# Recurrent mixer: triangular solve as 32x32 products joined by slot parity, low-rank products as 64x64 quarters in slots 33 and 35

## What is computed

```python
def rwkv_prepare(z, shift_w, w0, w_up, a0, a_up, k_k, k_a):
    ...
    w_log = -jax.nn.softplus(-(w0[:, None, None, :] + jnp.einsum('btr,drc->dbtc', jnp.tanh(wd), w_up))) - 0.5
    decay = jnp.exp(-jnp.exp(w_log.astype(jnp.float32)))
    a = jax.nn.sigmoid(a0[:, None, None, :] + jnp.einsum('btr,drc->dbtc', ad, a_up))
    ...
def wkv_scan(s0, scan_in):
    def step(s, inp):
        w, kk, a, k, v, r = inp
        sa = jnp.einsum('dbhij,dbhj->dbhi', s, kk)
        s = s * w[..., None, :] - sa[..., :, None] * (kk * a)[..., None, :] + v[..., :, None] * k[..., None, :]
        return s, jnp.einsum('dbhij,dbhj->dbhi', s, r)
    return lax.scan(step, s0, scan_in)
```

## Time and profile before

| | us |
|---|---|
| median of 3 runs | 4435.7 |
| the runs | 4431.9, 4435.7, 4444.6 |
| profiled execution, own time | 4427.0 |
| its span | 4425.4 |
| `rwkv_phase` in it | about 2085 to 2800 |
| one iteration of it (2249.21 to 2292.39) | 43.2 |

### The profile page before, as it was taken

One profiled execution on the slowest core, in us unless ns is written; L12 is line 12 of the kernel. 1 busy time (PEld: TensorE's weight loads), 2 busy tenths in 40 slices (PEclk: granted clock), 3 DMA queues, 4 the chain that ended last, 5 costly groups with the idle time before them and its releaser, 6 DMA issues. The chain is left out here.

```text
span 4425.4 us, 76116 instructions
## 1 busy us (share of the span) xinstructions
PE 3997.9 (90%) x30302; PEld 2848.3 (64%) x30302; DVE 2760.9 (62%) x5967; ACT 1446.1 (33%) x3210; POOL 900.1 (20%) x926
## 2 busy tenths in 40 slices
PE   7989999998999899998999999898999777778777
PEld 6747887755788687787888888686444333333332
DVE  5674433665533566755666666245777888888885
ACT  3353342344523335712444444322111111111111
POOL 1101110110201101110000000101344444444443
PEclk9999999999999999999999999898999999999999
DMA  4203443311443310131000000434999999999998
GB/s 127 86 30 109 154 141 99 103 36 39 157 144 128 117 57 20 63 132 51 19 18 26 24 18 6 151 111 164 388 409 420 416 415 415 409 409 417 412 415 334
DMA packets 149522, 795.01 MB, mean 180 GB/s; under 512 B 18808, under 2 KB 22120, under 8 KB 82352
## 3 DMA queue, kind: packets, MB, share of 16 engines
q0 software_dynamic: 84560, 574.75, 32.2%
q1 hardware_dynamic: 57120, 188.06, 13.0%
q10 hardware_dynamic: 7488, 27.30, 1.9%
HBM read 765.84 MB, written 20.00 MB: 178 GB/s over the span
## 5 line engine op out<-in xcount | busy, mean ns | idle before, releaser
L3224 PE MATMUL psum<-rows,diag 128*128 128x512 f32 x2048 | 1007.3, 642 | 226.7 <-ACT diag L3103 207.7
L3224 PEld LDWEIGHTS psum<-rows,diag 128*128 128x128 f32 x2048 | 410.4, 205 | 779.5 <-issue 765.9
L2922 POOL DMA_INDIRECT rows<-in_peer_uv,sel_idx x512 | 612.6, 1197 | 739.7 <-PE psum L3224 675.4
L2965 DVE SCALAR_TENSOR_TENSOR uh<-rows,h_rows 128x1024 f32<-128x1024 f32 x512 | 628.1, 1227 | 208.1 <-DMA rows<-in_peer_uv,sel_idx 183.1
L529 DVE TENSOR_TENSOR w_split_lo<-w_raw,w_split_hi 128x1024 fp32r<-128x1024 f32 (+1 forms) x271 | 326.2, 1214 | 497.6 <-ACT w_split_hi L516 493.2
L516 ACT CAST w_split_hi<-w_raw 128x1024 fp32r<-128x1024 f32 (+1 forms) x271 | 276.4, 1027 | 621.4 <-PE psum L465 396.7
L3096 ACT ACTIVATE g<-g 128x4 f32<-128x4 f32 x128 | 26.3, 205 | 1092.5 <-DVE g L2976 1092.5
L693 POOL TENSOR_TENSOR uT_lo<-normed_rows,uT_hi 128x512 fp32r<-128x512 f32 x64 | 90.2, 1410 | 661.2 <-ACT uT_hi L669 661.2
L465 PE MATMUL psum<-hT_mlp_hi,w_split_hi 128*128 128x512 f32 x512 | 201.3, 393 | 5.5 <-DVE hT_mlp_lo L261 5.5
L465 PE MATMUL psum<-hT_mlp_lo,w_split_hi 128*128 128x512 f32 x512 | 200.2, 391 | 0.0
L465 PE MATMUL psum<-hT_mlp_hi,w_split_lo 128*128 128x512 f32 x512 | 200.2, 391 | 0.0
(11 more groups left out here) (523 smaller groups left out, 8465.6 us busy)
## 6 DMA issues: line engine op xcount, KB each, us to landing
w_raw<-in_w_in SPq DMA_DIRECT2D x105, 512.0 KB, 4.1
w_raw<-in_w_up SPq DMA_DIRECT2D x64, 512.0 KB, 4.5
w_raw<-in_w_down SPq DMA_DIRECT2D x64, 512.0 KB, 4.4
amask_sb<-in_w_mod ACTq DMA_DIRECT2D x48, 512.0 KB, 3.7
wq<-in_peer_wq SPq DMA_DIRECT2D x24, 512.0 KB, 7.9
rows<-in_peer_uv,sel_idx POOLq DMA_INDIRECT x512, 12.6
qkpad<-in_w_out SPq DMA_DIRECT2D x12, 512.0 KB, 5.5
w_raw<-in_w_out SPq DMA_DIRECT2D x12, 512.0 KB, 4.3
```

What stands on the lines that cost most here:

```text
L2922: nc.gpsimd.indirect_dma_start(out=rows[:, n % RB, :], out_offset=None, in_=I["peer_uv"], in_offset=bass.IndirectOffsetOnAxis(ap=sel[:, t, ...
L2965: nc.vector.scalar_tensor_tensor(prod[:], rows[:, n % RB, 0:D], 1.0, h[:, t, :], ALU.mult, ALU.mult, accum_out=dots[:, (n // BATCH) % 2, s ...
L3224: last = nc.tensor.matmul(psum[:, 2 * (t % 2) + half, :], diag[:, n % (2 * BATCH), :], rows[:, n % RB, D + half * NB:D + (half + 1) * NB], ...
```

## The change

- `by_quarter` replaces `by_head` in levels 1 to 4 of the solve: only the two 32x32 diagonal blocks of each 64x64 product are computed, by 4 matmuls a chunk instead of 2. `across` does so for level 5, with 2 matmuls of 32x32 a chunk.
- TensorE's and ScalarE's order within a slot depends on the slot's parity: in odd slots `solve`, `scan`, `fill`, the rest; in even slots `fill`, the rest, `scan`, `solve`. So the solves of an even slot and the odd slot behind it stand next to each other. VectorE's order is as before, except for the decays below.
- The low-rank products are 8 matmuls of 64x64 (`quarter`), for unit `i+2`, in slots 33 and 35, in PSUM banks 7 and 3; ScalarE's tanhs stand there too.
- VectorE's three decay operations stand in slots 0, 1, 2 (before: 2, 3, 4), ScalarE's three exponentials in 3, 6, 9 (before: 7, 8, 9).

```diff
+    def by_quarter(out, lhsT, rhs):
+        for j, at in enumerate(quarters):
+            own = quarters[j % 2]
+            last = nc.tensor.matmul(out[at, own], lhsT[at, own], rhs[at, own], start=True, stop=True)
+        return last
+    def across(out, lhsT, rhs, source, target, mine, others):
+        for h in range(2):
+            rows = quarters[2 * h + source]
+            last = nc.tensor.matmul(out[quarters[2 * h + target], others], lhsT[rows, mine], rhs[rows, others],
+                                    start=True, stop=True)
+        return last
...
+                def quarter(w, col):
+                    return nc.tensor.matmul(psum[halves[col], (7, 3)[w], 0:hi - lo], up[halves[w], w, d, halves[col]],
+                                            lora[halves[w], lo:hi], start=True, stop=True)
+                quarter(0, 0)
+                quarter(1, 1)
+                quarter(0, 1).then_inc(lora_up, 1)
+                quarter(1, 0).then_inc(lora_up, 1)
...
                 for k in range(SLOTS_):
-                    if build is not None:
+                    if build is not None and k % 2:
                         solve(k, build)
-                        if 3 <= k < 12:
-                            fill(k, build)
-                    if scanned is not None:
+                    if scanned is not None and k % 2:
                         scan(k, scanned)
-                    if prep and k in (0, 2, 4, 6):
-                        lora_product(k, prep)
+                    if build is not None and 3 <= k < 12:
+                        fill(k, build)
+                    if factors and k in FACTORS_AT:
+                        lora_products(FACTORS_AT.index(k), factors)
                     if tile is not None:
                         tile_product(k, tile, prep)
...
+                    if scanned is not None and k % 2 == 0:
+                        scan(k, scanned)
+                    if build is not None and k % 2 == 0:
+                        solve(k, build)
...
-            def prepare(k, u):
-                g, d = divmod(u, 2)
+            def decays(k, u):
...
-                if k == 2:
-                    dve.wait_ge(opened, 4 * u + 2)
+                if k == 0:
+                    dve.wait_ge(opened, 4 * u + 3)
```

More of the change, by code:

```diff
@@ L1914, in rwkv_phase @@
     halves = (slice(0, 64), slice(64, P))
+    quarters = tuple(slice(32 * j, 32 * j + 32) for j in range(4))
     def cells(ap):
@@ L1959, in stages @@
         final = (i - MERGE) // 2 if i % 2 == ODD and i >= MERGE else None
-        return build, scan, prep, norm, tile, final
+        factors = i + 2 if i + 2 < UNITS else None
+        return build, scan, prep, norm, tile, final, factors
     ITERATIONS = range(-1, UNITS + 2)
@@ L2017, in _ @@
             for i in ITERATIONS:
-                build, scanned, prep, norm, tile, final = stages(i)
+                build, scanned, prep, norm, tile, final, factors = stages(i)
                 if prep:
@@ L2094, in solve @@
                         c = 4 * b + i
-                        last = by_head(psum[:, b, i * L_CH:(i + 1) * L_CH], AT[:, c], X[:, c], True, True)
+                        out = psum[:, b, i * L_CH:(i + 1) * L_CH]
+                        if lv < LEVELS:
+                            last = by_quarter(out, AT[:, c], X[:, c])
+                        else:
+                            last = across(out, AT[:, c], X[:, c], d, 1 - d, quarters[1 - d], quarters[d])
                     last.then_inc(u_ready, 1)
@@ L2190, in lora_product @@
                 else:
[L2191 to L2193 removed]
+                    pe.wait_ge(opened, 4 * u + 2)
+                def quarter(w, col):
[5 more added lines that the diff above has]
+                quarter(1, 0).then_inc(lora_up, 1)
             def head_sums(out, of):
@@ L2564, in _ @@
             norms(11, 0)
-            for k in (2, 3, 4):
-                prepare(k, 0)
+            for k in range(3):
+                decays(k, 0)
             norms(25, 0)
@@ L2579, in _ @@
                         bonuses(k, tile)
-                    if prep is not None and (prep or k > 4):
+                    if prep:
+                        decays(k, prep)
+                    if prep is not None:
                         prepare(k, prep)
```

74 lines of the change are left out of this document (41 added, 33 removed).

## The result

| | before | after |
|---|---|---|
| median | 4436.3 us | 4635.1 us |
| runs | 4431.9 to 4444.6 | 4628.2 to 4643.6 |
| profiled execution, own time / span | 4427.0 / 4425.4 | 4629.6 / 4627.9 |

A forecast was written before the change was run, and what follows sets the result against it. It took TensorE as packed, with chain waits hidden by work between links. Slots 0 to 12 (29), 12 to 33 (5), 33 to 36 (25) and clock (20) gave +79: 4515 us, forecast 4480 to 4560, range 4448 to 4640.

The forecast's parts named there:

- clock term: Behind new TensorE waits the granted clock halves: some 18 places, three quarters at 1.5 us, +20, bounds 0 and +27.
- Unit prices: TensorE: a 32x32 solve product takes 0.25 us instead of 0.47; a pair of size changes costs 0.255.
- Slots 0 to 4: TensorE's turned b in slot 4 waits for VectorE's `BT_cells` readout, whose chain grows from 5.7 to 7.2 us: +1.5.
- Slots 4 to 12: Cheaper solve and departed low-rank products against size changes and waits whose cover moved away: +0.4 us in total.
- Slots 12 to 33: Solve savings against size changes and uncovered scan waits: -0.4 us in even iterations, +1.15 in odd ones.
- Slots 33 to 36: Low-rank quarters and tanhs ahead of N's copy stretch W to the next Gram product from 1.74 to 3.6 us: +1.9.
- Sum without the clock: Whole kernel: slots 0 to 12 give 29 us, slots 12 to 33 give 5, slots 33 to 36 give 25.
- The rival with a floor: Records cannot start closer than 29 ns, so levels 1 to 4 cost 0.93 a product: +240, 4755; chance 0.14.
- halfway case: Floor rival at 14.5 ns a record: about +90, 4605, where the prediction put that rival; chance 0.14.
- Size changes nearly free: Rival: TensorE's tile size changes cost nearly nothing and the clock holds: +10 to +35, 4460; chance 0.08.
- TensorE's work decides: Rival: waits stay covered, so only TensorE's own sum counts: -5.2 us an iteration, -75, 4360; chance 0.13.

The follow-up runs named there:

- VectorE order experiment: After, with `fill` ahead of `solve` and `turn` in VectorE's slots 3 to 11: 4606.8 us, ratio to before 1.0383.
- the move: Before, with only the low-rank products as quarters in slots 33 and 35, decays in slots 0 to 2, exponentials in 3, 6, 9: 4487.4 us, ratio 1.0101.
- the one run that changed little but the clock: After, with eight unread 64x64 products of 512 columns put into TensorE's slot 4 wait: 4615.1 us, ratio to before 1.0400.

## Why the prediction was right and wrong

The prediction had the direction, the prices and the places of the waits right. The step that failed is its clock term, +20, with bounds 0 and +27, where some 79 us are the estimate from the runs; and it had no term for the supply of instructions, where the runs show gaps of 37.5 to 42.6 us. That 4635 still fell inside the range is luck: the upper bound stood there for a floor on records that the trace refutes.

- **Unit prices: right.** A 32x32 product 0.28 (0.25), a pair of size changes 0.27 (0.255), four quarters at once in the low-rank products.
- **Slots 0 to 4: right.** 7.1 us behind the first readout, TensorE idle 3.3 to 3.6. Putting the decays later took most of the wait away and gave 67 us back, which the +1.5 an iteration doesn't show; the step counted only the lengthening of the path, not the clock that an idle TensorE pays.
- **Slots 4 to 12: right in place, somewhat low.** Forecast waits 0.68, 1.44, 0.68 and 1.1; read between starts 0.84 (slot 6), 1.36 (slot 7), 0.69 (slot 8), 1.13 (slot 10). The VectorE order experiment shows the cause of the second.
- **Slots 12 to 33.** W to N waits 0.53 (0.52), and the last steps' wait is 14.3 us in 7 times against 7.0, that is +1.04 (+1.0).
- **Slots 33 to 36: right.** 3.6 us (3.6), by the tanhs.
- **Sum without the clock: right where it applied.** Some 57 to 62 us against 59; as a remainder it is only as good as the two estimates taken off. Iterations cleaned of gaps and clock are 47.0 and 48.4 us (47 and 48). Outside the stretch the prediction had next to nothing, +1 for two iterations together, and 24 us were measured. The first iteration alone took 14.5 more, with the clock at 0.63; the other 9.4 no run explains.
- **The clock: the term that was mis-sized.** It had "some 18 new places, three quarters at 1.5", +20, bounds 0 and +27. Measured: 31 pieces, 198 us, so 6.4 us a piece instead of the 3.3 of the earlier trace rows, and some 79 us for the 188 us that are new. Two errors lie in it. I took one length of a fall from one row. And I counted 13 or 14 falls where 28 are new, since I looked at waits of other engines only, while gaps that I did not know of let it fall as well. The waits' share shows in after with the 64x64 solve: 85 us at the lower level, without any gap.
- **The supply of instructions: the term that was missing.** 37.5 to 42.6 us. The prediction weighed whether records can start densely, but not whether they arrive densely. The record counts were there to be had from the order of the changed kernel: 36,574 of TensorE for 30,302.
- **The rival with a floor** said 4605 and 4755 and would have been nearest. Its mechanism is refuted: 32 records do start in 0.28 us. It was right that more records cost more than their columns, by another road. Its halfway case is also added up too high: 0.21 more for 22 products in 15 iterations is some +70, not +90.
- **Size changes nearly free**: refuted by the 0.27. The sum for it is off too: taking 15 pairs at 0.255 in 14 iterations from the 59 leaves some +5, not +10 to +15.
- **TensorE's work decides**, 4360: refuted by the waits. That the merged parts could pay is shown in a smaller frame, by the quarters in slots 0 and 2.

**Parts and whole.** Alone, the quartered solve costs 93, the order 104 and the move 49, together 246; the whole costs 199. Parity order and the move share the slot 4 wait (16.8 and 46.4 us alone, 47.7 together), and each part alone lets the clock fall in stretches that another would have slowed anyway. I have not divided the 47 further.

**What is shown of the gaps, and what stays open.** They lie within groups and without semaphores, they end a fixed time behind the packets of the instruction queue, they occur in all five kernels with quartered levels 1 to 4, and level 5 alone in 32x32 does not bring them. The other seven kernels have none above 0.6 us, the 14 waits for ScalarE's tanhs aside; there the shortest time in which TensorE goes through 256 instructions is 3.7 us. What leaves no rival is the place: all 161 gaps above 0.6 us of the five kernels stand at the same place of a 256-instruction block (number 233 to 235 modulo 256). A wait of another kind would not keep to it. Open is why a packet takes as long as it does: no run made the fetch faster or varied the number of instructions with the tiles left at 64x64. Open too is the clock's full size. The 79 us rest on the rates above, and the one run that changed little but the clock gave 20 us.

## What to carry to other kernels

Count instructions as well as columns: when a product is cut into twice as many small ones, its price in starts can be right and the engine still stop for want of instructions, so look whether the stretch can spare 1 to 1.5 us pauses. The number to compare is a block of 256 instructions, weight loads counted: the seven kernels without such gaps never went through one in under 3.7 us, and where the others starved a block took 3.8 to 3.9 us on average, while two quartered solve products one behind the other are 128 instructions in 0.6 us. And price a new wait of TensorE with the clock that falls behind it, by the length of falls in several rows: here 2.5 us of idle an iteration, taken away, gave back nearly as much again. A product cut into parallel tiles pays where its results are awaited late and its readers stand before nothing urgent, as slots 0 and 2 show against 33 and 35.

## What was unexpected of the hardware

- TensorE stopped 32 times in 827 us for 37.5 us with no semaphore to wait for, in a kernel with groups of 32 records in 0.28 us, and each time at the same place of a block of 256 instructions. Packets of 16 KB, one such block each, came every 3.3 to 8.7 us there (median 4.2), lasted 0.9 to 1.5 us, and a gap ended 1.24 to 1.54 us behind one. The kernel before has a packet every 3.4 to 7.6 us (median 4.9) and no gaps.
- The clock fell behind gaps of 0.3 to 1.5 us in the midst of dense work (11 of 13 falls in the kernel with only the quartered solve), and stayed at 1.2 GHz for 6.4 us on average in after.
- Adding 8 products of 512 columns to each unit made the kernel 20 us faster.
